# Pooling products of a decoder layer in three one-pass matmuls, with their operands split on ScalarE and VectorE

## The reference

```
n      = rmsnorm(x);  proj = n @ w_in             # columns: pool 512 | lru 512 | gate 512
y_pool = pool_mixer(pool columns)
xc     = causal_conv4(lru columns);  r, i = sigmoid gates of xc
a      = exp(-8 r softplus(-lam));  h_t = a_t h_(t-1) + sqrt(1 - a_t^2) i_t xc_t
mix    = [rmsnorm(y_pool), rmsnorm(h * gelu(gate columns))]
x      = x + mix @ w_out;  x = x + swiglu_ffn(rmsnorm(x));  out = rmsnorm(x)

pool_mixer: for g, w in ((0, 2), (1, 4), (2, 8), (3, 16)):     # 128 channels each
    d_g = (mean of the last w tokens of u_g) - u_g
    y_g = (d_g @ pool_w[g]) * pool_scale_g
```

## Time and profile before

| | |
|---|---|
| median of 3 runs | 912.07 us (911.73 to 912.11) |
| the profiled execution's own time | 911.77 us |
| its span in the profile | 910.0 us |
| PE busy | 893.8 us, 98% |
| DVE busy | 602.6 us, 66% |
| ACT busy | 390.0 us, 43% |
| POOL busy | 272.4 us, 30% |
| mean granted TensorE clock | 0.997 |

### The profile page before, as it was taken

One profiled execution on the slowest core, in us unless ns is written; L12 is line 12 of the kernel. 1 busy time (PEld: TensorE's weight loads), 2 busy tenths in 40 slices (PEclk: granted clock), 3 DMA queues, 4 the chain that ended last, 5 costly groups with the idle time before them and its releaser, 6 DMA issues.

```text
span 910.0 us, 10954 instructions
## 1 busy us (share of the span) xinstructions
PE 893.8 (98%) x3956; PEld 729.8 (80%) x3956; DVE 602.6 (66%) x835; ACT 390.0 (43%) x647; POOL 272.4 (30%) x211
## 2 busy tenths in 40 slices
PE   7999999999999999999999999999999999999996
PEld 5777777888888788888888888888888888888885
DVE  5678895644679855575655656647557975787666
ACT  6679524532565432333323333233325444445455
POOL 1000012534243754555446555464550000000000
PEclk9999999999999999999999999999999999999998
DMA  9010102114010223332233322333229943333324
GB/s 317 8 47 27 43 24 70 48 47 139 0 46 25 81 93 127 93 128 82 93 128 92 128 82 93 128 93 127 81 93 350 406 122 94 103 94 96 100 82 185
DMA packets 93678, 95.91 MB, mean 105 GB/s; under 512 B 5636, under 2 KB 63544, under 8 KB 93624
## 3 DMA queue, kind: packets, MB, share of 16 engines
q1 hardware_dynamic: 83240, 76.32, 24.8%
q10 hardware_dynamic: 10384, 18.88, 7.0%
HBM read 70.81 MB, written 24.38 MB: 105 GB/s over the span
## 4 chain that ended last, share of the span: by engine, by line
PE 95%; DVE 2%; DMA 1%; ACT 1%; POOL 0%; issue 0%; SPq 0%; DVEq 0%; ACTq 0%
PE bank L1835 23%; PE bank L1837 23%; PE bank L1836 23%; PE bank L1721 4%; PE bank L1723 4%; PE bank L1722 4%; PE bank L1665 3%; PE bank L1667 3%; PE bank L1666 3%; PE bank L1740 2%; DMA h<-in_x 1%; PE bank L1751 1%; PE bank L1699 1%; DVE nT_lo L1178 1%; DVE xc L1256 0%; PE bank L1758 0%
## 5 line engine op out<-in xcount | busy, mean ns | idle before, releaser
L653 POOL TENSOR_TENSOR r_lo<-gu_raw,r_hi 128x512 fp32r<-128x512 f32 x84 | 116.8, 1391 | 68.4 <-ACT r_hi L920 68.3
L653 POOL TENSOR_TENSOR r_lo<-wsum_S,r_hi 128x512 fp32r<-128x512 f32 x63 | 98.7, 1567 | 125.2 <-ACT r_hi L920 125.2
L1835 PE MATMUL bank<-T_hi,r_lo 128*128 128x512 f32 x336 | 130.9, 390 | 0.9 <-DVE u L1521 0.9
L1837 PE MATMUL bank<-T_hi,r_hi 128*128 128x512 f32 x336 | 130.7, 389 | 0.0
L1836 PE MATMUL bank<-T_lo,r_hi 128*128 128x512 f32 x336 | 130.7, 389 | 0.0
L1835 PE MATMUL bank<-d_hi,h_lo 128*128 128x512 f32 x308 | 119.8, 389 | 0.0
L1836 PE MATMUL bank<-d_lo,h_hi 128*128 128x512 f32 x308 | 119.8, 389 | 0.0
L1837 PE MATMUL bank<-d_hi,h_hi 128*128 128x512 f32 x308 | 119.8, 389 | 0.0
L920 ACT CAST r_hi<-gu_raw 128x512 fp32r<-128x512 f32 x84 | 52.2, 621 | 131.2 <-PE bank L1837 131.2
L1835 PE MATMUL bank<-nT_hi,r_lo 128*128 128x512 f32 x252 | 98.1, 389 | 0.0
L1836 PE MATMUL bank<-nT_lo,r_hi 128*128 128x512 f32 x252 | 98.0, 389 | 0.0
(11 more groups left out here) (214 smaller groups left out, 1619.3 us busy)
## 6 DMA issues: line engine op xcount, KB each, us to landing
h_raw<-hid_ops ACTq DMA_DIRECT2D x72, 256.0 KB, 2.6
gu_raw<-in_w_ffn_gate SPq DMA_DIRECT2D x22, 512.0 KB, 3.7
gu_raw<-in_w_ffn_up SPq DMA_DIRECT2D x22, 512.0 KB, 4.8
hid_ops<-hid SPq DMA_DIRECT2D x44, 256.0 KB, 2.2
dn<-in_w_ffn_down SPq DMA_DIRECT2D x44, 256.0 KB, 9.8
hid_ops<-hsum_S SPq DMA_DIRECT2D x33, 256.0 KB, 2.5
w_raw<-in_w_in SPq DMA_DIRECT2D x11, 512.0 KB, 3.8
h<-in_x SPq DMA_DIRECT2D x8, 512.0 KB, 6.8
```

Of the source, the lines that this page charges most:

```text
L653: pool.tensor_tensor(lo_of(n)[:], a_block(f, name), f32(hi_of(n)[:]), ALU.subtract)\
L1835: pe.matmul(bank, s_lo, m_hi, start=(opens and j == 0), stop=False, skip_group_check=True)
L1837: ins = pe.matmul(bank, s_hi, m_hi, start=False, stop=(closes and j == n - 1), skip_group_check=True)
```

## The change

The pooling products become three-pass products like the others. For that the pooling weights (128x512) and the difference of each group (128x1024) are split. The high parts are casts on ScalarE into new tiles: `pw_hi`, and `pd_hi` with two buffers. The low parts are subtractions on VectorE, written over the unsplit tiles (`pw_lo` over `pool_ws`, `pd_lo` over `xc`). Two of the new places overlap old ones: `pd_hi` 0 lies in the last quarter of `y[0]`, and `pd_hi` 1 where the recurrence's `t2b` is, so that it waits for the last scan.

Places in the order: on ScalarE the weights' cast stands at the end of step 4, the first difference's cast in `decay` of the last recurrence, between tanh and exp, and those of groups 1 to 3 in steps 6 to 8 behind the squares of the group before, ahead of `evacuate(c, 1)`. On VectorE the weights' and the first difference's low parts stand in step 5 between `first_half(5)` and the last `recur`, and those of groups 1 to 3 in steps 6 to 8 behind `pool_output`, ahead of `window_mean` (steps 6 and 7) or `gate_lru` (step 8). `pool_product(p)` waits for `pd_lo_ok` in place of `d_ok`. No transfer is added or moved.

```diff
+            def pool_weights_hi():
+                act.wait_ge(small_in, 16 * 5)
+                act.wait_ge(rb_ok, 1)
+                act.copy(pw_hi[:], pool_ws[:]).then_inc(pw_hi_ok, 1)
+            def pool_hi(p):
+                act.wait_ge(d_ok, p + 1)
+                if p == 1:
+                    act.wait_ge(scan_ok, GT)
+                if p >= 2:
+                    act.wait_ge(poolmm_ok, 2 * (p - 1))
+                act.copy(pd_hi[p % 2][:], xc[p % 2][:]).then_inc(pd_hi_ok, 1)
...
                 act.activation(t2, rg[:], ACT.Tanh, scale=sp[:, 6, j:j + 1]).then_inc(t2_ok, 1)
+                if j == GT - 1:
+                    pool_hi(0)
                 act.activation(ag[:], rg[:], ACT.Exp, scale=sp[:, 7, j:j + 1]).then_inc(a_ok, 1)
...
                     pool_squares(c - POOL0 - 2)
+                if 1 <= c - POOL0 - 1 < GT:
+                    pool_hi(c - POOL0 - 1)
...
                 evacuate(c, 1)
+                if c == POOL0:
+                    pool_weights_hi()
...
+            def pool_weights_lo():
+                dve.wait_ge(pw_hi_ok, 1)
+                dve.tensor_tensor(pw_lo[:], pool_ws[:], f32(pw_hi[:]), ALU.subtract).then_inc(pw_lo_ok, 1)
+            def pool_lo(p):
+                dve.wait_ge(pd_hi_ok, p + 1)
+                dve.tensor_tensor(pd_lo[p % 2][:], xc[p % 2][:], f32(pd_hi[p % 2][:]), ALU.subtract).then_inc(pd_lo_ok, 1)
...
                     first_half(c)
+                if c == POOL0 + 1:
+                    pool_weights_lo()
+                    pool_lo(0)
                 if 0 <= c - 2 < GT:
                     recur(c - 2)
                 if 0 <= c - POOL0 - 2 < GT:
                     pool_output(c - POOL0 - 2)
+                if 1 <= c - POOL0 - 1 < GT:
+                    pool_lo(c - POOL0 - 1)
...
             def pool_product(p):
-                pe.wait_ge(d_ok, p + 1)
+                pe.wait_ge(pw_lo_ok, 1)
+                pe.wait_ge(pd_lo_ok, p + 1)
...
-                    pe.matmul(pg[w % 2][:], pool_ws[:, p], xc[p % 2][:, half(i)], start=True, stop=True)\
-                        .then_inc(poolmm_ok, 1)
+                    three_pass(pg[w % 2][:], [(pw_hi[:, p], pw_lo[:, p], pd_hi[p % 2][:, half(i)],
+                                               pd_lo[p % 2][:, half(i)])]).then_inc(poolmm_ok, 1)
```

More of the change, by code:

```diff
@@ L108, in hymba_pool_rglru_block @@
         sq_scr = at("sq_scr", 196.25, [P, 512])
+        pw_hi, pw_lo = at("pw_hi", 200.5, [P, GT, P], F32R), at("pw_lo", 188.25, [P, GT, P], F32R)
+        pd_hi = [at(f"pd_hi{s}", (164.25, 148.25)[s], [P, S], F32R) for s in range(2)]
+        pd_lo = [at(f"pd_lo{s}", 120 + 4 * s, [P, S], F32R) for s in range(2)]
         xs2 = [at(f"xs2_{s}", 116 - 4 * s, [P, D]) for s in range(2)]
@@ L237, in hymba_pool_rglru_block @@
         psq_ok = sem("psq_ok")
+        pw_hi_ok, pw_lo_ok, pd_hi_ok, pd_lo_ok = (sem(n) for n in ("pw_hi_ok", "pw_lo_ok", "pd_hi_ok", "pd_lo_ok"))
         lsq_ok = sem("lsq_ok")
```

## The result

The changed kernel takes 916.0 us (median of 6 runs, 915.36 to 916.61) against 911.92 us of the kernel before: a ratio of 1.0046 with a 95% interval of 1.0036 to 1.0056, 4.1 us slower. The forecast was 916.3 with a range from 913.6 to 918.2. The profiled execution has a span of 914.4 us, 4.4 more than before.

What follows compares the result with a forecast made beforehand. TensorE, busy 893.8 of 910.0 us, bounds the kernel; late splits delay the fourth product by 4.7 us, less 0.4 saved there: 4.3 over 911.77 or 912.07, forecast 916.3, range 913.6 to 918.2.

Steps and rivals of the forecast that it cites:

- What the matmuls save: Each pooling group on TensorE: 1.72 us of fp32 matmuls become 1.36; 0.40 us saved by whole period, 1.6 for four.
- all hidden: Rival: low parts are never late, above all at the second product; the kernel wins its 1.6 us, 910.5; chance 0.05.
- Column 5: First difference: its cast between tanh and table load makes ScalarE's exp and root 0.95 us later; TensorE does not wait.
- The cover for VectorE's additions: Column 5: VectorE's wait for the root hides its added subtractions; without it up to 1.9 us more would show.
- Column 6: Second difference: cast behind the squares, subtraction until 119.57; second product at 119.7 for 116.81, TensorE idle 3.4 us.
- Column 7: Third difference: subtraction held to 131.7, VectorE 3.3 us later; TensorE idle 0.8 us ahead of column 9's projection.
- Column 8: Fourth difference: subtraction held until 145.7, ends 146.8; fourth product at 146.9 for 142.17; rest of kernel 4.3 us later.
- The hold: GpSimd's adds of squares lengthen VectorE's third and fourth subtraction; worth 2.6 us of the 4.3.
- the case without a hold: Rival: GpSimd holds neither the third nor fourth subtraction; sum +1.7, near 913.8; chance 0.09.
- The clock: Rival: idle 3.4 us ahead of second product halves TensorE's clock; up to 2.7 us lost stays hidden; visible loss chance 0.11.
- the rule that spoke against the step: At the hold: GpSimd blocks VectorE only in two-port modes, fp32 on two tensors uses none; by that alone +1.7.

## Why the prediction was right

The time came out 4.1 us up against 4.3 forecast, and most steps of the chain were hit:

- *What the matmuls save.* 1.36 us a group was right. That the four are worth 1.6 us was used in two places. In the sum it did no harm, since it was counted at the fourth product alone and the rest went into waits, which the run with fp32 products confirms. As the price of the rival "all hidden", 910.5, it was too good: the matmuls without any split gain 1.0. The step that failed there is that I took the kernel before to have room on VectorE once the links are gone. It waited already at the second product (0.11 and 0.19 us), and those rows should have told me that the first group's gain would only lengthen that wait.
- *Column 5.* Shift 0.95 forecast, 0.96 and 0.97 in the trace (root; squares at 116.10 for 115.13). The cover for VectorE's additions held: it still waited 0.74 us for the root.
- *Column 6.* Second product forecast at 119.7, found at 119.66.
- *Column 7.* Third subtraction forecast to end at 131.7, ended at 131.71. But TensorE was to reach the third product at 131.9 and start column 9 after a wait of 0.8 us. It reached the product at 133.64, and there was no such wait: the clock, below, took its place.
- *Column 8.* Fourth product forecast at 146.9, found at 146.89.
- *The hold.* Forecast at 2.6 us of the 4.3. Both adds cut short give 0.9 us alone. With TensorE kept busy they give 2.64 between the first and the fourth product, and 2.9 by the times (916.26 and 913.41), so the size was right for a clock that stays. Behind a clock that falls, the case without a hold would have come out at 915, not at 913.8 as my rival had it: I priced each rival with the others absent.
- *The clock.* The rival in which it falls behind the second product and is hidden is what happened: 1.7 us lost, the wait ahead of column 9 gone, the one ahead of the fourth product 0.9 us shorter. The sum didn't change: idle 3.34 and 1.01 us by the starts of matmuls and 1.74 lost by the clock are 6.1, as are the 3.4, 0.8 and 1.9 forecast. I had worked out that up to 2.7 us would be hidden, but no row told me that the stretch would be as short as 3.4 us; a longer one would have shown, and to that extent the number is luck. Keeping TensorE busy shows it from the other side; the waits then are 0.52 and 1.61. I had forecast 0.8 and 1.9 by the starts of matmuls; the brackets count from the end of the last matmul (0.39 us after its start, where the next would start after 0.23) and so show 0.16 less, and the rest is rounding. The 3.18 of the second product is 3.34 by starts, against 3.4.

As for the rule that spoke against the step: the sentence of the Trainium skill on VectorE Performance Modes in "Advanced Engine Details and Errata", by which an operation on two tensors would not be held, doesn't fit the 2.68 and 2.60 us that became 1.23 with the short adds. The sentence of the Trainium skill in "SBUF — State Buffer", section Who interferes with whom, by which an operation with two SBUF inputs contends with a GpSimd instruction that reads SBUF, does.

## What to carry to other kernels

Before adding a split in front of a matmul, follow the queue of the engine that makes it: here 1.2 us of VectorE per group, in a stretch where it was nearly full, cost more than the 0.4 us that TensorE saved, and the same work ordered by who waits first gained 1.9 us over the kernel before. When an engine is late as a whole, moving one of its consumers only moves the wait to the next one; move every operation that somebody waits for ahead of those that nobody waits for. Test delays that end at the same wait together, since one alone can show 0 to 0.9 us of the 2.6 that both are worth.

## What the runs showed of the hardware

- Whether the clock falls isn't settled by the length of the idle stretch alone. It fell behind 3.18 us of idle TensorE in the changed kernel and behind 2.07 in the one with the splits moved up, and stayed at 1.00 through 2.81 us in the one with the products moved back (the profiled execution of each; executions of one kernel can differ, as the times and mean clocks of the last two suggest). The half rate lasted from about 120.6 to 124.0 in the changed kernel and cost 1.7 us. The Trainium skill ("TensorE: Matmul & The Clock Gate", section Why this matters for your kernels) warns of idle gaps between bursts of matmuls. The first two agree; the third shows such a gap without a fall.
- GpSimd's add of 1024 columns holds an operation of VectorE with two SBUF inputs that starts after it: the window sum and the gate product of the kernel before and the third and fourth subtraction of the changed one ended 1.07 to 1.09 us behind the add. The operations out of PSUM beside it (the outputs at 127.52 and 142.68, of which the second of each pair overlaps the add) kept their 1.53 us for two.
